# Raw latent tiles: the first projection starts from x times the norm's weights, with the norm beside it and the loads in another order

## The reference

```python
def rmsnorm(x, g):
    xf = x.astype(jnp.float32)
    y = xf * lax.rsqrt(jnp.mean(xf * xf, axis=-1, keepdims=True) + EPS)
    return (y * g.astype(jnp.float32)).astype(x.dtype)
...
    h = rmsnorm(x, norm_mix_g)
    proj = jnp.einsum('bsd,de->bse', h, w_in)
    (c_q, c_kv, k_r, q_b, k_b, v_b, q_i, k_i, w_i, g_a, g_b) = jnp.split(proj, splits, axis=-1)
    c_q = rmsnorm(c_q, mla_q_norm_g)
    q_a = jnp.einsum('bsr,re->bse', c_q, w_uq)...
    c_kv = rmsnorm(c_kv, mla_kv_norm_g)
```

## Time and profile before

| | us |
|---|---|
| median of 3 runs | 2105.24 (2101.94 to 2108.37) |
| the profiled execution, its own time | 2096.68 |
| its span, first to last instruction | 2094.9 |

### The profile page before, as it was taken

One profiled execution on the slowest core, in us unless ns is written; L12 is line 12 of the kernel. 1 busy time (PEld: TensorE's weight loads), 2 busy tenths in 40 slices (PEclk: granted clock), 3 DMA queues, 4 the chain that ended last, 5 costly groups with the idle time before them and its releaser, 6 DMA issues. The chain is left out here.

```text
span 2094.9 us, 36833 instructions
## 1 busy us (share of the span) xinstructions
PE 1936.0 (92%) x14716; PEld 1659.6 (79%) x14716; DVE 1322.9 (63%) x2057; ACT 906.1 (43%) x1384; POOL 705.6 (34%) x381
## 2 busy tenths in 40 slices
PE   7999999998899998699999996888899999999998
PEld 4787836675687876599999876788589999999786
DVE  2678758433799898589992674655421468887413
ACT  4324238433788887522233552253233343333313
POOL 2433300231021211243445312330145455555443
PEclk9999999999899999799999988999799989999998
DMA  5222210122999998223223214120132222222221
GB/s 186 90 81 77 85 61 2 51 86 97 404 363 379 367 371 322 98 92 122 91 91 113 81 41 126 29 37 8 42 132 91 81 79 85 98 85 99 71 100 51
DMA packets 91313, 260.08 MB, mean 124 GB/s; under 512 B 26320, under 2 KB 29536, under 8 KB 90528
## 3 DMA queue, kind: packets, MB, share of 16 engines
q1 hardware_dynamic: 87424, 247.90, 33.3%
q0 software_dynamic: 3744, 10.11, 1.4%
HBM read 239.10 MB, written 18.87 MB: 123 GB/s over the span
## 5 line engine op out<-in xcount | busy, mean ns | idle before, releaser
L1744 DVE TENSOR_TENSOR moe_wlo<-moe_ring,moe_whi 128x1024 fp32r<-128x1024 f32 x198 | 233.1, 1223 | 39.4 <-ACT moe_whi L1740 38.4
L562 PE MATMUL acc<-h_xhi,h_whi 128*128 128x264 f32 x816 | 234.2, 287 | 7.0 <-DVE h_xlo L462 3.7
L562 PE MATMUL acc<-h_xhi,h_wlo 128*128 128x264 f32 x816 | 234.1, 287 | 0.0
L562 PE MATMUL acc<-h_xlo,h_whi 128*128 128x264 f32 x816 | 233.8, 286 | 0.0
L401 POOL TENSOR_TENSOR h_wlo<-ring,h_whi 128x1024 fp32r<-128x1024 f32 x59 | 141.5, 2399 | 245.5 <-ACT h_whi L392 245.3
L1740 ACT ACTIVATE moe_whi<-moe_ring 128x1024 fp32r<-128x1024 f32 x198 | 205.9, 1058 | 41.2 <-PE acc L1801 21.6
L562 PE MATMUL acc<-ff_xhi,ff_wlo 128*128 128x258 f32 x672 | 190.7, 284 | 0.0
L562 PE MATMUL acc<-ff_xhi,ff_whi 128*128 128x258 f32 x672 | 190.7, 284 | 0.0
L562 PE MATMUL acc<-ff_xlo,ff_whi 128*128 128x258 f32 x672 | 190.1, 283 | 0.0
L562 PEld LDWEIGHTS acc<-h_xhi,h_whi 128*128 128x128 f32 x816 | 155.7, 191 | 8.5 <-DVE h_xlo L462 4.1
L2311 DVE SCALAR_TENSOR_TENSOR acc<-cp,par,acc 128x528 f32<-128x528 f32 x232 | 159.4, 769 | 0.0
(11 more groups left out here) (545 smaller groups left out, 5081.1 us busy)
## 6 DMA issues: line engine op xcount, KB each, us to landing
ring<-slabs SPq DMA_DIRECT2D x213, 512.0 KB, 3.5
moe_ring<-moe_slabs SPq DMA_DIRECT2D x204, 512.0 KB, 6.4
tok_rows<-h_tok SPq DMA_DIRECT2D x5, 512.0 KB, 4.1
h_spill<-x2r SPq DMA_DIRECT2D x1, 2112.0 KB, 9.3
v_spill<-rw_v SPq DMA_DIRECT2D x1, 2112.0 KB, 7.4
y_spill<-cp SPq DMA_DIRECT2D x8, 264.0 KB, 4.0
x2r<-h_spill SPq DMA_DIRECT2D x1, 2112.0 KB
x2r<-y_spill SPq DMA_DIRECT2D x1, 2112.0 KB
```

What stands on the lines that cost most here:

```text
L562: mm = nc.tensor.matmul(acc[j][0:rows, s, 0:t1 - t0], wp[:, at:at + rows], xp[:, t0:t1], start=(k == 0 and m == 0), stop=(k == kt - 1 and ...
L1744: tensor_tensor(wlo[u % AHEAD][:, :], ringm[u % RAW][:, :], whi[u % AHEAD][:, :].bitcast(F32), ALU.subtract).then_inc(w_lo[u % 2], 1)
```

## The change

The block `normalize("mix", ...)` is gone. Its work stands inside the first block of `attention_part`, beside the projection, and the five latent tiles are computed from x * norm_mix_g (the operand `raw`), without the factor `mix_rstd` of each token. The latent norms that follow take that factor out again: a token's c_q comes out larger by s = sqrt(mean(x^2) + 1e-6), and its norm gives the same as before if its epsilon is multiplied by s^2. So DVE makes `c_eps_of` = 1e-6 * s * s once and adds it to the two sums of squares, where before ACT's root had a constant epsilon as bias. The tiles from 5 on use h as before.

```diff
-        def load_slabs(sp, name=None):
+        def load_slabs(sp, name=None, stop=RING):
...
                 def load(sp):
+                    load_slabs(sp, stop=1)
+                    sp.dma_start(par[:, :], params_d).then_inc(loaded, 16)
+                    for k in range(KD):
+                        if k == 4:
+                            load_slabs(sp, stop=2)
+                        sp.dma_start(xt[:, k, :], x_t[:, k, :]).then_inc(x_here[k], 16)
                     sp.dma_start(c0[:, :], const0).then_inc(c0_here, 16)
-                    for k in range(KD):
-                        sp.dma_start(xt[:, k, :], x_t[:, k, :]).then_inc(x_here[k], 16)
-                    sp.dma_start(par[:, :], params_d).then_inc(loaded, 16)
                     load_slabs(sp)
                     sp.dma_start(c1[:, :], const1).then_inc(c1_here, 16)
                     sp.wait_ge(loaded, 16)
+                    sp.wait_ge(c0_here, 16)
...
-                    normalize("mix", lambda k: xt[:, k, :], lambda k: h[:, k, :], KD, T1, k0("mean1024"),
-                              None, left=mix_rstd, enter=(load, arrived), split=(in_w, "c_q"))
...
+                raw = Operand(px, "raw", KD, T1, hi=Tiles([raw_tile("hi", k, qk_at + 4 * T1 * k) for k in range(KD)]),
+                              lo=Tiles([raw_tile("lo", k, (qi_at if k < 4 else vb_at) + 4 * T1 * (k % 4)) for k in range(KD)]))
...
+                        def behind(j):
+                            if j:
+                                late(j - 1)
+                            if j == 1:
+                                pe.wait_ge(c0_here, 16)
+                                pe.wait_ge(x_summed, 1)
+                                nc.tensor.matmul(acc[0][:, 1, :], k0("mean1024"), h[:, 0, :], start=True, stop=True).then_inc(ms_ready, 1)
...
-                            pe_tiles(pe, w, name, KD, n, hx, T1, tile_ready, tile_out,
-                                     rows=96 if name == "k_r" else P, first=i, then=lambda j: late(j - 1) if j else None)
+                            pe_tiles(pe, w, name, KD, n, raw if i < FIRST_ROPE else hx, T1, tile_ready, tile_out,
+                                     rows=96 if name == "k_r" else P, first=i, then=behind)
...
                     def _(act):
-                        w.begin(act, ["c_q"], hx)
...
+                        act.wait_ge(dummy_set, 1)
+                        nc.scalar.activation(c_eps_of[:, 0:1], mix_rstd[:, 0:1], ACT.Sqrt)
+                        first_slab = SLAB0["c_q"]
+                        w.act(act, first_slab)
+                        act.wait_ge(loaded, 16)
+                        for k in range(KD):
+                            act.wait_ge(x_here[k], 16)
+                            nc.scalar.activation(raw.hi[:, k, :], xt[:, k, :], ACT.Identity,
+                                                 scale=pcol("norm_mix_g", k)).then_inc(x_hi, 1)
+                            if k == 4:
+                                w.act(act, first_slab + 1)
+                        for k in range(KD):
+                            nc.scalar.activation(h[:, k, :], xt[:, k, :], ACT.Square).then_inc(x_squared, 1)
+
+                        def root(j):
+                            act.wait_ge(c_eps, j + 1)
+                            nc.scalar.activation(std(j), std(j), ACT.Sqrt).then_inc(c_root, 1)
...
+                            if i == 1:
+                                act.wait_ge(c0_here, 16)
+                                act.wait_ge(ms_ready, 1)
+                                nc.scalar.activation(mix_std, acc[0][:, 1, :], ACT.Sqrt, bias=k0("eps", 1, EPS_RMS)).then_inc(ms_rooted, 1)
+                            if i in (2, 3):
+                                hx.act(act, 4 * i - 8, 4 * i - 4)
...
                     def _(dve):
+                        nc.vector.memset(mix_rstd[:, 0:1], 1.0).then_inc(dummy_set, 1)
+                        dve.wait_ge(loaded, 16)
+                        for k in range(KD):
+                            dve.wait_ge(x_hi, raw.base + k + 1)
+                            nc.vector.scalar_tensor_tensor(out=raw.lo[:, k, :], in0=xt[:, k, :], scalar=pcol("norm_mix_g", k),
+                                                           in1=raw.hi[:, k, :].bitcast(F32), op0=ALU.mult,
+                                                           op1=ALU.subtract).then_inc(x_lo, 1)
+                        for k in range(1, KD):
+                            dve.wait_ge(x_squared, k + 1)
+                            ins = nc.vector.tensor_tensor(h[:, 0, :], h[:, 0, :], h[:, k, :], ALU.add)
...
+                        dve.wait_ge(ms_rooted, 1)
+                        link("dve", dve, nc.vector.scalar_tensor_tensor(out=c_eps_of, in0=mix_std, scalar=1e-6, in1=mix_std,
+                                                                        op0=ALU.mult, op1=ALU.mult))
+                        link("dve", dve, nc.vector.reciprocal(mix_rstd[:, :], mix_std))
                         hx.dve(dve)
+                        for j, n in enumerate((3, 5)):
+                            dve.wait_ge(c_summed, n)
+                            nc.vector.tensor_tensor(std(j), acc[2 + j][:, 1, :], c_eps_of, ALU.add).then_inc(c_eps, 1)
...
                     def _(sp):
+                        load(sp)
                         load_slabs(sp, "v_b")
```

More of the change, by code:

```diff
@@ L325, in slab_done @@
             mm.then_inc(slab_used, 1)
-        def load_slabs(sp, name=None):
+        def load_slabs(sp, name=None, stop=RING):
             if name is None:
-                stop = RING
+                pass
             else:
@@ L868, in first_block @@
                     in_w = Weights(in_ctx, "in", side="right")
-                    normalize("mix", lambda k: xt[:, k, :], lambda k: h[:, k, :], KD, T1, k0("mean1024"),
-                              None, left=mix_rstd, enter=(load, arrived), split=(in_w, "c_q"))
                     with ExitStack() as att:
-                        attention_part(att, mix, xt, h, k1, mix_rstd, c1_here, in_ctx, in_w, c1_at + 4 * C1["cos64"])
+                        attention_part(att, mix, xt, h, k1, mix_rstd, load, x_here, c0_here, c1_here, in_ctx, in_w, c1_at + 4 * C1["cos64"])
                 x1 = first.enter_context(nc.sbuf_tensor("x1_tok", [P, 4, D], F32, side="right"))
@@ L1004, in _, with attention_part @@
                     normal(3)
-        def attention_part(att, mix, xt, h, k1, mix_rstd, c1_here, in_ctx, w, tables_at):
+        def attention_part(att, mix, xt, h, k1, mix_rstd, load, x_here, c0_here, c1_here, in_ctx, w, tables_at):
             here = lambda: -(-nc.sbuf_base // 32) * 32
@@ L1011, in attention_part @@
             qi, ki = sbt(att, "qi", [P, 4, T1]), sbt(att, "ki", [P, T1])
+            vb_at = here()
             vb = sbt(att, "vb", [P, 4, 512])
@@ L1040, in attention_part @@
                 px.enter_context(in_ctx)
+                raw_tile = lambda part, k, at: nc.alloc_sbuf_tensor_at(f"raw_{part}{k}", [P, T1], F32R, offset=at)
+                raw = Operand(px, "raw", KD, T1, hi=Tiles([raw_tile("hi", k, qk_at + 4 * T1 * k) for k in range(KD)]),
+                              lo=Tiles([raw_tile("lo", k, (qi_at if k < 4 else vb_at) + 4 * T1 * (k % 4)) for k in range(KD)]))
+                raw.start(lambda k: xt[:, k, :])
                 hx = Operand(px, "in", KD, T1)
@@ L1049, in attention_part @@
                 wi_ready = sem("wi_ready", True)
+                x_summed, c_eps, x_squared, ms_ready, ms_rooted, dummy_set = norm_sems
+                norm_base[:] = [1, 2, KD, 1, 1, 1]
                 with block() as b:
+                    mix_std, c_eps_of = gb[:, 4, :], gb[:, 5, :]
                     sq = lambda i: gb[:, i % 4, :]
@@ L1099, in _ @@
                     def _(act):
-                        w.begin(act, ["c_q"], hx)
-                        def root(j, n):
-                            act.wait_ge(c_summed, n)
-                            nc.scalar.activation(std(j), acc[2 + j][:, 1, :], ACT.Sqrt, bias=k0("eps", 1, EPS_RMS)).then_inc(c_root, 1)
+                        act.wait_ge(dummy_set, 1)
[14 more added lines that the diff above has]
+                            nc.scalar.activation(std(j), std(j), ACT.Sqrt).then_inc(c_root, 1)
                         def take(i):
@@ L1115, in take @@
                                 nc.scalar.activation(sq(i), dests[i], ACT.Square).then_inc(c_sq, 1)
+                            if i == 1:
[4 more added lines that the diff above has]
+                                hx.act(act, 4 * i - 8, 4 * i - 4)
                             if i == 7:
-                                root(0, 3)
-                                root(1, 5)
+                                root(0)
+                                root(1)
                             if i == KR + 4:
@@ L1131, in _ @@
                     def _(dve):
+                        nc.vector.memset(mix_rstd[:, 0:1], 1.0).then_inc(dummy_set, 1)
```

(12 more changed lines are left out.)

## The result

| kernel | median us | lowest to highest | runs |
|---|---|---|---|
| before | 2106.82 | 2096.08 to 2111.24 | 7 |
| changed | 2092.31 | 2085.99 to 2101.55 | 7 |

The ratio is 0.9946 with a 95% interval of 0.9927 to 0.9965, which is 7 to 15 us faster. The forecast was 2093.2 in a range of 2085.5 to 2101.0, from a gain of 12.0 us. Two things in the trace are not as forecast: tile 5 comes 10.5 us earlier, not 12.0, and the two profiled executions differ by only 4.4 us (2096.68 and 2092.31), not by 10.5. The rest of this document is about these two.

What follows compares the result with a forecast made beforehand. DVE was taken to pace the first tile, PE everything after. Tile 0 ending 13.0 us earlier, less 0.86 for the added matmul and 0.1 of waiting, gave 12.0; 2105.24 - 12.0 = 2093.2 us, range 2085.5 to 2101.

Steps and rivals of the forecast that it cites:

- PE is the limit once it starts, and the block hands its gain on: From tile 1 to the block's end PE sets the pace, 6.46 us per later tile; time won earlier is passed on whole.
- The transfers: Start of the block: reordered loads land along the old trace's bytes-against-time curve, x0 at 8.2 us, PE starting at 9.65.
- The low parts beside POOL: In tile 0, POOL's work on slab 1 blocks DVE's low parts of x5 to x7, the last ending at 18.4 us.
- The clock: In tile 0's 2.4 us wait for x5: no extra cost, since the clock had outlived 5 us of idleness.
- slower start: Rival: x up to 2 us later, or PE at half speed early in tile 1 (1.8 us); 2095 to 2097, chance 0.14.
- The wait ahead of tile 2: PE's matmul over x's squares needs DVE's seven additions, one held by POOL's slab 2; PE waits only 0.1 us.
- What is late next: Before tile 5: h's last low part at 45.8 us leaves 5 us of cover, slab 6 has 4; no cost.
- Cover gone: Rival: the chain to h slips over 5 us, PE waits at tile 5 or 6; 2099 to 2105, chance 0.09 including no effect.
- the change does not do what it says: Rival: PE's first matmul still waits for the norm; no gain, 2105, within the 0.09 for cover gone or no effect.
- the second pass: Rival: changed rounding shifts routing, a group's count crosses 128, all eight groups rerun for 294 us; 2387, chance at most 0.02.
- faster start: Rival: loads miss the curve's slow part and low parts escape POOL; tile 5 gains 14.7 us, time 2090.5, chance 0.11.

## Why the prediction was right, and where it was off

**PE is the limit once it starts, and the block hands its gain on.** Right: PE's periods from tile 3 on are 6.45 to 6.48 us, against 6.46 before, and 10.51 us arrive at tile 5 and at the block's end.

**The transfers.** The curve of the earlier trace rows gave x0 at 8.2; ACT began on it at 6.98. PE started at 8.72, not 9.65. The curve was too slow there. With the old order the same reasoning gave 17.6 for PE's start, and 17.53 was measured. In the new order the end of tile 0 was hardly moved by it (18.6 instead of 19.2), because that end hangs on x5, slab 1 and POOL.

**The low parts beside POOL.** Right: 3.69 us for three, against 2.85 for four without POOL (slab 1 rounded later).

**The clock.** This step failed in its reason. A wait in tile 0 was called harmless because the clock had outlived 5 us of idleness in the earlier trace rows. In three profiles that share the beginning (changed twice, additions left out; waits of 1.15, 0.89 and 2.06 us) it was harmless, although the new cold start lasted to 14.8 in one of them. In the fourth (x's norm one tile later) the same wait, 1.84 us by the profile, was followed by 3.8 us at the low level, which cost 1.6 us (16.09 to 25.47 from there to the first latent sum, against 16.40 to 24.23). It is the "slower start" rival, in one of four executions and near its price of 1.8. The length of the wait does not decide it, as 2.06 us were harmless and 1.84 were not; what does is open. The same happened behind the wait of 2.52 us for L1084 with slab 1 rounded later, for the same 1.6 us. So the 5 us of the earlier trace rows, behind 8.7 us of steady work, were no measure for these waits.

**The wait ahead of tile 2.** This term was mis-sized, and it is the miss that matters: 0.1 us was forecast, about 1.9 measured (PE was free at 25.09 and L1084 came at 26.97). The forecast let POOL hold up one addition; POOL did slabs 2 and 3 back to back, from 20.37 to 25.55, since ACT finished its squares earlier (0.53 us each, not 0.65) and had both slabs rounded before DVE was through. With tile 0 ending 0.6 earlier, this wait 1.8 longer, and 0.3 more between L1084 and tile 2's eviction (6.75 instead of 6.46), tile 5 comes at 51.6 - 0.6 + 1.8 + 0.3 = 53.1, as measured. Of these 0.3, 0.2 are a slip of the sum: it set PE's end of tile 0 (19.2) against an eviction (32.2), and an eviction starts 0.2 us behind the matmul that follows the tile (33.72 behind 33.52).

**What is late next.** Right: the last low part of h at 46.76 (forecast 45.8), no wait for it, 5 us of cover. That the cover is real and not much larger is shown by x's norm one tile later: h's last low part came 4.7 us later and had 0.8 us left. What ran out there first was the slabs' cover (forecast at 4 us for slab 6, and not named for slab 5): POOL has slab 5 at 42.28 in the changed kernel, and at 46.95 in that one.

**The rivals.** "Cover gone", "the change does not do what it says" and the second pass did not occur; "faster start" was half met in the transfers and not at all in POOL. The median fell within 1 us of the forecast, though the sum was 1.5 us too large; with runs spread over 15 us that closeness is luck. The two medians of the result lie 14.5 us apart, the ratio says 11.4 and the trace 10.5.

## What to carry to other kernels

A normalization whose result is only normed again can be left out ahead of a product and put back through the epsilon; its gain is PE's earlier start, and more than half of it came only with loads in the order in which the new beginning needs them, an order that was a loss by itself. When DVE works with two SBUF inputs beside POOL's subtractions, count how many of POOL's instructions fall into the stretch, not how many DVE instructions: seven additions took 9.2 us beside two slabs, 10.6 beside three and 12.7 beside four, which is about 2 us for each on top of some 4.9 alone (an estimate: seven times the 0.69 us that one took by itself). And look at what waits for the blocked instruction first: here moving POOL's work alone gained nothing, moving the consumer (PE's matmul) gained 1.3 us. Compare stages of two profiles only after looking at how far the same stage lies apart in two profiles of one kernel.

## What the runs showed of the hardware that was not expected

The recorded clock does not show the start. Two stretches of PE in the changed kernel, with the clock behind the busy time:

```profile
8.00:14.00 6.00, 5.28 (x13) 1.00 1.04 404
...
15.00:20.00 5.00, 3.85 (x17) 1.00 1.01 418
```

The record gives 1.00 for both, but 13 matmuls fit into the 6 us of the first and 17 into the 5 us of the second in spite of its wait: the steps were 0.43 us until 14.8 and 0.23 after. By its steps PE was at the low level from its first matmul on, which the record does not say before the clock's first change. Later falls are recorded: with slab 1 rounded later the clock is 0.91 in the stretch from 27 to 28 us and 0.50 from 28 to 31, so that it fell when PE had resumed (27.29), not in the wait. How long the low level lasts after PE begins was not a matter of the code: it was 3.6 us with six additions left out (8.63 to 12.2) and 6.1 in the changed kernel's first profile (8.72 to 14.8), with the same instructions up to there. And the same kernel's recurrence stage takes 297 to 310 us with a mean granted clock of 0.89 to 0.86, which is the largest part of what lies between the two profiles of before (12.9 of 17.1 us).
